# Second mixer's input projection by seven block products, split in two token halves and joined with the output stage before it

## What is computed

```python
    x = x + (o * jax.nn.silu(g)) @ w_out_b[j]
return _rmsnorm(x, norm_f)
```

```python
    h = rms_norm(x, norm_w[l]) * (1.0 + scale[:, None, :]) + shift[:, None, :]
    proj = jnp.einsum('bsd,de->bse', h, w_in[l])
    u_pool, g_pool, q, k, v, g_attn, qi, ki, wi = jnp.split(proj, split_points, axis=-1)
    pool_out = pool_mixer(u_pool, w_pool[l], pool_scale[l]) * jax.nn.silu(g_pool)
    q = rope(rms_norm(q.reshape(B, S, N_HEADS, HEAD_DIM), q_norm_w[l]), pos)
    k = rope(rms_norm(k.reshape(B, S, N_KV_HEADS, HEAD_DIM), k_norm_w[l]), pos)
    qi = rope(qi.reshape(B, S, N_IDX_HEADS, IDX_DIM), pos)
    ki = rope(ki[:, :, None, :], pos)[:, :, 0, :]
```

## Time and profile before

| | |
|---|---|
| median of 3 runs | 3083.36 us (3082.87 to 3084.82) |
| span of the profiled execution | 3082.3 us |
| matmuls on PE, busy | 2955.2 us, 96% |
| DVE busy | 2238.4 us, 73% |
| ACT busy | 1631.1 us, 53% |
| POOL busy | 297.2 us, 10% |

### The profile page before, as it was taken

One profiled execution on the slowest core, in us unless ns is written; L12 is line 12 of the kernel. 1 busy time (PEld: TensorE's weight loads), 2 busy tenths in 40 slices (PEclk: granted clock), 3 DMA queues, 4 the chain that ended last, 5 costly groups with the idle time before them and its releaser, 6 DMA issues. The chain is left out here.

```text
span 3082.3 us, 48442 instructions
## 1 busy us (share of the span) xinstructions
PE 2955.2 (96%) x17512; PEld 2368.1 (77%) x17512; DVE 2238.4 (73%) x3267; ACT 1631.1 (53%) x2923; POOL 297.2 (10%) x683
## 2 busy tenths in 40 slices
PE   6999999999999999999999999999978899999899
PEld 5888888888878886777777888888756667777687
DVE  8888887766576758889879665535278998888553
ACT  5343422232454546777769534222278899988510
POOL 2000000000000001000100000000022333333100
PEclk8999999999999999999999999999978999999999
DMA  4434422257755423111127334232551111111774
GB/s 123 125 106 119 159 73 69 69 184 246 217 172 139 176 99 115 32 29 56 46 68 234 98 118 137 98 124 77 156 117 42 25 37 24 26 39 41 166 223 139
DMA packets 375235, 334.66 MB, mean 109 GB/s; under 512 B 97275, under 2 KB 328187, under 8 KB 368973
## 3 DMA queue, kind: packets, MB, share of 16 engines
q1 hardware_dynamic: 368676, 294.73, 33.4%
q0 software_dynamic: 5600, 36.51, 3.4%
...
## 5 line engine op out<-in xcount | busy, mean ns | idle before, releaser
L349 ACT ACTIVATE s_mx_w_hi<-s_mx_raw 128x512 fp32r<-128x512 f32 x224 | 138.5, 628 | 310.1 <-PE p_oa_acc L705 238.2
L705 PE MATMUL p_oa_acc<-s_h_a_hi,s_mx_w_hi 128*128 128x512 f32 x744 | 291.5, 392 | 8.5 <-DVE s_h_a_lo L448 7.1
L705 PE MATMUL p_oa_acc<-s_h_a_lo,s_mx_w_hi 128*128 128x512 f32 x744 | 290.4, 390 | 0.0
L705 PE MATMUL p_oa_acc<-s_h_a_hi,s_mx_w_lo 128*128 128x512 f32 x744 | 290.4, 390 | 0.0
L1821 DVE TENSOR_TENSOR_SCAN s_st_prod<-s_st_soft,s_st_prod 128x512 f32<-128x512 f32 x192 | 234.9, 1269 | 8.3 <-ACT s_st_soft L1748 7.6
L1748 ACT ACTIVATE s_st_soft<-p_st_z 128x512 f32<-128x512 f32 (+3 forms) x320 | 153.4, 533 | 108.5 <-PE p_st_z L1874 107.7
L3565 PE MATMUL p_sa_turn<-s_ident,s_sa_arg 128*128 128x128 f32 x1088 | 164.9, 287 | 42.2 <-ACT s_sa_prob L3163 22.7
L491 DVE TENSOR_TENSOR s_mx_w_lo<-s_mx_raw,s_mx_w_hi 128x512 fp32r<-128x512 f32 x224 | 153.5, 686 | 53.6 <-ACT s_mx_w_hi L349 52.1
L2654 PE MATMUL p_pr_ps<-s_h_hi,s_pr_w_hi 128*128 128x512 f32 (+1 forms) x680 | 183.1, 390 | 1.2 <-DVE s_pr_w_lo L2509 1.0
L2654 PE MATMUL p_pr_ps<-s_h_hi,s_pr_w_lo 128*128 128x512 f32 (+1 forms) x680 | 182.9, 389 | 0.0
L2654 PE MATMUL p_pr_ps<-s_h_lo,s_pr_w_hi 128*128 128x512 f32 (+1 forms) x680 | 182.9, 389 | 0.0
...
## 6 DMA issues: line engine op xcount, KB each, us to landing
s_mx_raw<-in_w_in_a SPq DMA_DIRECT2D x128, 256.0 KB, 3.9
...
s_pr_work<-s_pr_stage SPq DMA_DIRECT2D x38, 256.0 KB, 4.4
d_rot_hi<-s_pr_rot POOLq DMA_DIRECT2D x9, 1024.0 KB, 4.3
d_rot_lo<-s_pr_stage POOLq DMA_DIRECT2D x9, 1024.0 KB, 6.3
...
```

Of the source, the lines that this page charges most:

```text
L705: ins = nc.tensor.matmul(bank, w[:, m, k, :], a[:, m, k, :], start=(k == 0 and n == 0), stop=(k == KH - 1 and n == 2))
```

## The change

Both stages become one block; each engine first runs its `out_b` program, then its `rotate` program, with no barrier between.

- The 2048 tokens are taken as two halves of 1024. For each half and each pair of 128-column blocks (a "group", 256 columns) seven products are made for eight: 7 x 4 channel blocks x 3 passes are 84 matmuls of 512 tokens. A half has one "tail" group (the 72 columns of ki and wi, four plain products, 48 matmuls) and 11 whole groups: norm and pool alternate four times, then norm (k with v), then two of gates. The second half begins with its own tail. A norm group holds q rows and a gate block, a pool group holds a window block and a qi block; so the post-processing of `order` is kept, in halves of 1024 tokens, each done while PE works on the group behind.
- The seven weight blocks of a group ([128, 4, 128]) come from four loads and four sums, now on POOL (`sum`); ACT makes the seven high parts, DVE the seven low parts. Both halves load and split their weights anew.
- Products add up in three PSUM regions; four copies by ACT (`first`, `p5`, `u2`, `u3`) keep what a running sum holds at that point, DVE forms two quadrants of 512 from PSUM and a copy (`leave_b`, `leave_c`), ACT copies one (`leave`), and POOL adds one (`finish`). PE waits for these copies between products.
- In the output stage the tiles come in the order `ROWS` (0, 4, 1, 5, ...). POOL takes the gating and the four sums of token blocks (`sum_up`) for the first half; ACT and DVE split 14 pieces of 1024 elements instead of 16 tiles. Tiles of the second half go to memory (`rows_late`), are loaded back at group `LAST` (the last of the first half), and are summed and split (3 sums of 2048 elements and 7 splits on DVE, 1 sum on POOL) during `LAST`, `LATE` (the tail) and the group behind it. PE fills the last tiles' passage with the 48 matmuls of the first tail.
- All stores move from POOL's queue to SP's. Buffers move to other places, and the copy of attention outputs back in `phase_stick` waits for two stored pieces instead of one.

The core of the diff:

```diff
-                    xt = halves(inner, "h_2")
...
-                    phase_out_b(nc, sem, out_space, x1, o_t, kvqg_t, a["norm_f"], ident, xf, first_r, *xt, xt_raw, a["w_in_2"][0][:, ROW_Q:ROW_Q + P], first_ps)
-                space.before_rotation(Alloc(nc, third, "right"))
-                phase_project_rotate(nc, sem, a["w_in_2"][0], *xt, a["w_pool_2"][0], a["pool_scale_2"][0],
...
+                out_b = out_b_programs(nc, sem, out_space, pairs, x1, o_t, kvqg_t, a["norm_f"], ident, xf, rows_late, ps, pt)
+                rotate = rotate_programs(nc, sem, a["w_pool_2"][0], a["pool_scale_2"][0], a["cos_t"], a["sin_t"], a["inv_count"], p_t, mix_t,
+                                         rot_hi, rot_lo, rows_late, first_r, space, out_space, pairs, ps, pt)
+                phase_out_b_rotate(nc, out_b, rotate)
...
+class Seven:
+    A11_B11, S1_T1, S2_T2, A12_B21, S3_T3, S4_B22, A22_T4 = range(MULTS)
...
+def column_groups(half):
+    groups = [Columns("tail", half, ROW_KI, None, None, None)]
+    for n in range(4):
+        groups.append(Columns("norm", half, ROW_Q + P * n, ROW_GP + P * n, 0, None))
+        groups.append(Columns("pool", half, ROW_U + P * n, ROW_QI + P * n, None, n))
+    groups.append(Columns("norm", half, ROW_K, ROW_V, 1, None))
+    groups += [Columns("gates", half, ROW_GA + P * n, ROW_GA + P * n + P, None, None) for n in (0, 2)]
+    return groups
...
+    TAIL_PRODUCTS = ((S.A12_B21, S.A11_B11), (S.A12_B21, S.S1_T1), (S.S3_T3, S.A12_B21), (S.S3_T3, S.S4_B22))
...
+    def sum(self, nc, pool, g, n):
+        S, n_th, before, raw = self.S, self.whole(g) + 1, self.sums_before[g], self.raw
+        if n == 0:
+            pool.wait_ge(self.a_in["a21"], 16 * n_th)
+            pool.wait_ge(self.a_in["a22"], 16 * n_th)
+            self.slot_free(pool, g, S.S1_T1)
+            ins = nc.gpsimd.tensor_tensor(raw[S.S1_T1][:], self.a21[:], self.a22[:], ALU.add)
+        if n == 1:
+            pool.wait_ge(self.a_in["a11"], 16 * n_th)
+            pool.wait_ge(self.summed, before + 1)
+            self.slot_free(pool, g, S.S2_T2)
+            ins = nc.gpsimd.tensor_tensor(raw[S.S2_T2][:], raw[S.S1_T1][:], raw[S.A11_B11][:], ALU.subtract)
+        if n == 2:
+            ins = nc.gpsimd.tensor_tensor(self.a21[:], raw[S.A11_B11][:], self.a21[:], ALU.subtract)
+        if n == 3:
+            pool.wait_ge(self.a_in["a12"], 16 * n_th)
+            pool.wait_ge(self.summed, before + 2)
+            self.slot_free(pool, g, S.S4_B22)
+            ins = nc.gpsimd.tensor_tensor(raw[S.S4_B22][:], raw[S.A12_B21][:], raw[S.S2_T2][:], ALU.subtract)
+        ins.then_inc(self.summed, 1)
...
+    def split_lo(self, nc, dve, g, q):
+        S, before = self.S, self.sums_before[g]
+        dve.wait_ge(self.hi_done[q], self.nth(g, q))
+        last_reader = {S.A11_B11: 3, S.S1_T1: 2, S.S2_T2: 4, S.A12_B21: 4}.get(q)
+        if last_reader:
+            dve.wait_ge(self.summed, before + last_reader)
+        nc.vector.tensor_tensor(self.w_lo[q][:], self.raw[q][:], self.w_hi[q][:].bitcast(F32), ALU.subtract).then_inc(self.lo_done[q], 1)
...
+    def multiply(self, nc, pe, bank, q, opens):
+        for k in range(KH):
+            for n, (w, a) in enumerate(split_pass_list(self.w_hi[q][:], self.w_lo[q][:], self.x_hi[:, q], self.x_lo[:, q])):
+                ins = nc.tensor.matmul(bank, w[:, k, :], a[:, k, :], start=opens and k == 0 and n == 0, stop=k == KH - 1 and n == 2,
+                                       skip_group_check=not opens)
+        ins.then_inc(self.product, 1)
...
+    PIECES_AT = {9: 2, 10: 2, 11: 1, 12: 1, 13: 2, 14: 2, 15: 2, 16: 1, 17: 1}
...
+        def sum_up(i):
+            x, cols = pairs.x_raw, slice(i * P, i * P + P)
+            pool.wait_ge(shifted_act, len(BY_ACT) * (2 * i + 2))
+            pool.wait_ge(shifted_dve, len(BY_DVE) * (2 * i + 2))
+            nc.gpsimd.tensor_tensor(x[:, S.S1_T1, :, cols], x[:, S.S3_T3, :, cols], x[:, S.A11_B11, :, cols], ALU.subtract).then_inc(summed, 1)
+            nc.gpsimd.tensor_tensor(x[:, S.S3_T3, :, cols], x[:, S.S4_B22, :, cols], x[:, S.S3_T3, :, cols], ALU.subtract).then_inc(summed, 1)
+            pool.wait_ge(summed, 4 * i + 2)
+            nc.gpsimd.tensor_tensor(x[:, S.S2_T2, :, cols], x[:, S.S4_B22, :, cols], x[:, S.S1_T1, :, cols], ALU.subtract).then_inc(summed, 1)
+            pool.wait_ge(summed, 4 * i + 3)
+            nc.gpsimd.tensor_tensor(x[:, S.A22_T4, :, cols], x[:, S.A12_B21, :, cols], x[:, S.S2_T2, :, cols], ALU.subtract).then_inc(summed, 1)
+        nc.gpsimd.memset(eps, EPS).then_inc(ready, 1)
+        for i in range(TILES):
+            if EARLY <= i + 2 < TILES:
+                space.pool_gate(nc, pool, i + 2)
+            if i - 5 >= 0 and i % 2 and i - 5 < RESIDENT:
+                sum_up((i - 5) // 2)
...
+        def begin_next(n):
+            pe.wait_ge(added, TILES if n else TILES - 1)
+            pieces_done = len(pieces) // 2 + n + 1
+            pairs.tail_product(nc, pe, ps, 0, n, (pairs.x_hi_done, pieces_done), (pairs.x_lo_done, pieces_done))
+        pe.wait_ge(space.w_lo_done, AC)
+        for i in range(TILES):
+            multiply(i)
+            if i >= 2:
+                transpose(i - 2)
+        begin_next(0)
+        transpose(TILES - 2)
+        begin_next(1)
+        begin_next(2)
+        transpose(TILES - 1)
+        begin_next(3)
...
+        def finish(g):
+            whole = pairs.whole(g)
+            pool.wait_ge(pairs.u3_kept, whole + 1)
+            pool.wait_ge(pairs.p5_kept, whole + 1)
...
+            nc.gpsimd.tensor_tensor(lower[g % 2][:, PART:], pairs.u3[:], pairs.p5[:], ALU.add).then_inc(c22_made, 1)
...
+        def late_difference():
+            pool.wait_ge(late_in[2], 16)
+            pool.wait_ge(late_in[3], 16)
+            pool.wait_ge(product, pairs.before[LAST] + S.S3_T3 + 1)
+            nc.gpsimd.tensor_tensor(pairs.x_raw[:, S.S3_T3], ahead[1][:], ahead[0][:], ALU.subtract).then_inc(late_t3, 1)
...
+        for g in range(1, N):
+            nxt = g + 1
+            more = nxt < N and kinds[nxt] != "tail"
+            if more:
+                for n in range(3):
+                    pairs.sum(nc, pool, nxt, n)
+            if kinds[g] != "tail":
+                finish(g)
+            if g == LAST:
+                late_difference()
+            if more:
+                pairs.sum(nc, pool, nxt, 3)
...
+        def open_rest(g):
+            if kinds[g] == "gates":
+                act.wait_ge(b_left, g + 1)
+                act.wait_ge(c_left, pairs.whole(g) + 1)
+                nc.scalar.activation(upper[g % 2][:], upper[g % 2][:], ACT.Silu).then_inc(opened, 1)
+            if gate_lower(g):
+                act.wait_ge(c22_made, pairs.whole(g) + 1)
+                nc.scalar.activation(lower[g % 2][:, PART:], lower[g % 2][:, PART:], ACT.Silu).then_inc(opened, 1)
...
+        leave(N - 1)
+        open_rest(N - 1)
...
+        def leave_c(g):
+            dve.wait_ge(product, pairs.before[g] + S.S4_B22 + 1)
+            dve.wait_ge(pairs.u2_kept, pairs.whole(g) + 1)
+            nc.vector.tensor_tensor(upper[g % 2][:, PART:], pairs.bank_c(ps), pairs.u2[:], ALU.add).then_inc(c_left, 1)
...
+            if g == LATE:
+                late_sum(S.A22_T4)
+                late_low(2)
+            if whole:
+                if g == LATE + 1:
+                    late_low(4)
+                for q in (S.S2_T2, S.A12_B21):
+                    pairs.split_lo(nc, dve, g, q)
+            if was_kind == "norm":
+                low_squares(was)
+            if whole:
+                pairs.split_lo(nc, dve, g, S.A22_T4)
+            if was_kind == "pool":
+                low_mix(was)
+                add_windows(was)
+            if g == LATE:
+                late_low(3)
+            if was_kind in ("norm", "tail"):
+                times_sin(was)
+            if whole:
+                pairs.split_lo(nc, dve, g, S.S4_B22)
+                if g == LATE + 1:
+                    late_low(5)
+            if was_kind in ("norm", "tail"):
+                times_cos(was)
+                add_turned(was)
+            if was_kind == "pool":
+                low_pooled(was)
+            if was_kind == "norm":
+                invert(was, 0)
+                invert(was, 1)
+            if was_kind == "pool":
+                times_sin(was)
+                times_cos(was)
+            if whole:
+                leave_b(g)
+            if was_kind == "norm":
+                invert(was, 2)
+            if was_kind == "pool":
+                add_turned(was)
+            if g == LATE + 1:
+                late_low(6)
+            if g == LAST:
+                late_sum(S.S1_T1)
+                late_sum(S.S2_T2)
+                late_low(0)
+            if more and g:
+                pairs.split_lo(nc, dve, nxt, S.S1_T1)
+            if was_kind == "norm":
+                invert(was, 3)
+                times_inverse(was)
+            if more and g:
```

(57 more changed lines are left out.)

1532 lines of the change are left out of this document (937 added, 595 removed).

## The result

The changed kernel takes 3106.74 us (median of 4 runs, 3103.51 to 3112.17), the kernel before on the same chip 3083.11 (3078.80 to 3084.82). The ratio is 1.0078, its 95% interval 1.0066 to 1.0091: slower by 24 us, where 3064 was forecast and the range ended at 3100. The forecast's rival on the other side said 3109.

The account below looks back on a forecast made before the run. PE was taken as the bound, busy for nearly all of both stages. Terms -60.2 + 22 + 9 + 6 + 1 + 2.5 = -19.7 us, against the median 3083.4, gave 3064 us, range 3034 to 3100.

Parts of the forecast that it names:

- rival on the other side: DVE with POOL becomes the bound in the 16 norm and pool groups; 3109 us, chance 18%.
- fewer matmuls: Projection: 1944 matmuls for 2208, 264 fewer at 0.228 us each, 60.2 us less.
- pairs: Norm group then pool group: PE waits for DVE's late low parts, 11 us a half, 22 in all; bounds 5 and 55.
- turn: Start of the second half: PE waits for its tail behind DVE's and POOL's work, 9 us; bounds 3 and 14.
- output stage: Steps 9 to 12: DVE's added pieces and meetings with POOL cost 6 us; bounds 0 and 13.
- seam: Output stage to projection: barrier saves 1 us, first whole group's low parts may cost 2; +1, bounds -1 and 4.
- end: After the last product: three SiLUs instead of one, and two stores; 2.5 us, bounds 0.5 and 4.
- mixing, by window: Pool groups: PE waits for the pooled rows' low part 0, 1.2, 3.0 and 4.8 us, growing with the window.
- Reciprocals not longer: Sign of being right: DVE's reciprocals in norm groups keep their length beside POOL's sums.
- POOL's sums near 1.8 us: Sign of being right: POOL's additions, 1.27 us alone, have a mean near 1.8 us.
- the walk: Timeline from the start of the group behind a norm group: low squares 4.3 us, A11 20.6, PE wanting it at 20.1.
- Its sign: Sign of being wrong: idle time spread over all seven products, meaning DVE is the bound everywhere.

Follow-up runs that it names:

- the first run: Changed kernel with POOL's four sums of weight blocks a group replaced by memsets; first to last product copy 479.1 us for 508.7, totals not comparable.
- e3_fill: Changed kernel with unused matmuls filling PE's waits ahead of squares, mixing and second tail; the total moved by 0.3 us.
- e16_spread: Repaired kernel (inverse root on ACT, reordered, POOL's turn subtraction delayed; 3073.2 us) with only the output stage's x pieces spread over steps; won 3.0 us.
- the best version: Same repaired kernel (3073.2 us) with output-stage gates and additions on DVE, additions and pieces spread over steps; 3068.1 us, 0.9944 of the kernel before.

## Why the prediction was wrong, step by step

The terms of its sum beside what the trace of the changed kernel shows (PE's idle time by gap, and the half clock by matmul):

```
                          predicted   measured
fewer matmuls             -60.2       -59.9
pairs                      22         32 idle
turn                        9         11 idle
output stage                6         18 (13.7 idle more, 4.4 half clock)
seam                        1         4 (two gaps, at 1734 and 1757 us; one of 1.1 before)
end                         2.5       3.3
half clock, projection      none      11
sum                       -19.7       +21.5 measured; the rows add up to +19, 2 us are in no gap
```

**Right.** The matmuls: their number, and their pace in running groups (0.227 us). The largest waits: mixing, by window, none for the smallest, then 1.6, 3.4, 5.6 in the first half for the forecast 1.2, 3.0, 4.8 (less in the second half); the turn at 11 for 9; the end. Reciprocals not longer. POOL's sums near 1.8 us. That DVE and POOL take turns, and that it speaks against moving sums to POOL. The trace agrees with the Trainium skill there ("SBUF — State Buffer", Who interferes with whom): it also says that a GpSimd instruction that only writes does not contend, which the memsets of the first run show (703 ns for 915).

**Failed: the output stage, 6 us for 18.** The step looked for waits in steps 9 to 12 alone and said of the earlier ones that "POOL's meetings fit in what DVE lost". They did not. Three gaps of 1.6, 2.3 and 2.1 us from start to start end at 1643.7, 1658.7 and 1675.1. The first two lie ahead of every piece (ACT's first is at 1664.1, DVE's at 1674.7). Ahead of each of the three, POOL's additions and the gates behind them stretch DVE's product with the norm to 2.3 us for 1.22 and its low part to 1.78 for 0.68. Without the additions' reads one of the three is left, at 1.2 us, and the whole stage is 10 us shorter. So the overlap of POOL's work with DVE's chain was costed at nothing in steps where it made PE wait. A forecast could have asked how much the stage can take. Before the change DVE was busy for 65 of 66 us in its middle (107 of 123.5 over the whole stage). That this load by itself is a cause is argued, not shown, for in the changed kernel DVE also waits 19.6 us for PE in this stage.

**Failed: no term for the clock.** Both windows had 1.00, and the sum priced idle time as if it left the matmuls behind it as they were. Behind gaps of 2.2 to 6 us (not behind every one) PE's clock stands at 1.2 GHz. How much of it costs time depends on what bounds: in the projection filling the gaps gave back nothing (e3_fill), since DVE sets the pace. So the table's 11 us there are not a loss of their own: they are part of what DVE's lateness costs, and in effect the pairs and the turn cost more than the idle time in their rows. In the output stage no run gave back the clock alone; e16_spread, with nearly the same idle time at full clock, comes nearest.

**Mis-sized: the pairs, 22 for 32 idle.** The mixing waits lost 16.7 us for the forecast 18. The waits for A11 lost 6.6 for 4. The rest, 8.8 us, are seven waits for the squares of 0.8 to 2.3 us from start to start, and they were costed at nothing: the walk had DVE's low squares ready 4.3 us into the group and PE wanting them at 5.5, but DVE has them up to 2 us after that. The meetings were priced by one walk through one pair; the first run shows 29.6 us of PE's time for those with the sums of weights. (A smaller error: the four quarters of the reciprocal take 6.9 us, not the half of 12.95.)

The rival "DVE with POOL becomes the bound" had the mechanism and nearly the time, 3109. That the time fits so well is in part luck, for the split was wrong: 55 us in the pairs, against 32 and 11 of half clock, and 12 in the output stage, against 18. It was held at 18%, with the reciprocals and some idle time in every second group against it. The prediction's own sum spoke for it: DVE works 35.9 to 39.6 of PE's 40.6 us in a pair. On this reading a queue that is 88 to 98% full, and waits for ACT and PE besides, has no room for the 5 us that the sums' reads cost DVE in a pair (54 us over 21 groups). Its sign came as well: PE's idle time was not mostly ahead of the mixing product (17.8 of 69 us from start to start) but spread over A11, squares, mixing and the turn, and the two stages took 655 us for the 614 that were named.

**What stays open.** The turn (9 us of gaps in the best version), and the seam. Making POOL's sums of weights once and reading them back in the second half was not tried, nor were the sums of weights on DVE, the direct test of whether POOL is the wrong place for them.
